# Wider values' projection, an unrolled convolution stage, and h's two parts taken straight from PSUM

## The reference

```python
D_MODEL, SEQ, W_A, W_B, H_A, D_K, CONV_WIDTH = 2048, 512, 1024, 1024, 8, 128, 31
h = rmsnorm(x, pre_norm_g)                      # x: (1, 512, 2048) float32
proj = einsum('btd,dn->btn', h, w_in)           # w_in: (2048, 7168)
q, fz, iv, gate_a, u, ug, gate_b = split(proj)  # each 1024 wide; iv holds the values
o_a = hgrn2_mixer(q, fz, iv, lower_bounds, hg_norm_g) * silu(gate_a)
o_b = conformer_conv(u, ug, dw_kernel, dw_bias, conv_ln_g, conv_ln_b) * silu(gate_b)
y = einsum('btm,md->btd', concatenate([o_a, o_b]), w_out)
out = x + rmsnorm(y, post_norm_g)
```

## Time and profile before

| | us |
|---|---|
| three runs | 893.11, 890.41, 892.97 |
| median | 892.97 |
| the profiled execution, its whole time | 890.29 |
| its span in the profile | 888.3 |
| PE busy in it | 872.4 |
| mean granted clock of PE | 0.992 |

### The profile page before, as it was taken

One profiled execution on the slowest core, in us unless ns is written; L12 is line 12 of the kernel. 1 busy time (PEld: TensorE's weight loads), 2 busy tenths in 40 slices (PEclk: granted clock), 3 DMA queues, 4 the chain that ended last, 5 costly groups with the idle time before them and its releaser, 6 DMA issues.

```text
span 888.3 us, 13244 instructions
## 1 busy us (share of the span) xinstructions
PE 872.4 (98%) x4616; PEld 747.8 (84%) x4616; DVE 567.7 (64%) x911; ACT 386.7 (44%) x585; POOL 363.5 (41%) x165
## 2 busy tenths in 40 slices
PE   6999999999999999999999999999999999999996
PEld 5998898898898888888888888888888888888885
DVE  6877786786786894775849486684948892010105
ACT  6433312312312455654746565573756743222221
POOL 3374444444444444352442435244242534444440
PEclk8999999999999999999999999999999999999999
DMA  9243233233233233132232314233132345433304
GB/s 317 69 128 102 80 104 103 78 104 102 77 105 101 78 95 96 48 116 74 72 94 70 96 47 121 68 88 91 57 94 63 101 140 209 153 100 101 101 5 190
DMA packets 119703, 89.70 MB, mean 101 GB/s; under 512 B 2640, under 2 KB 109433, under 8 KB 118137
## 3 DMA queue, kind: packets, MB, share of 16 engines
q1 hardware_dynamic: 118921, 84.04, 31.1%
q10 hardware_dynamic: 752, 5.25, 1.6%
HBM read 85.09 MB, written 4.19 MB: 101 GB/s over the span
## 4 chain that ended last, share of the span: by engine, by line
PE 96%; DVE 3%; DMA 1%; ACT 0%; DVEq 0%; issue 0%; ACTq 0%
PE banks L1128 19%; PE banks L1126 19%; PE banks L1127 19%; PE banks L1268 7%; PE banks L1267 7%; PE banks L1266 7%; PE banks L1143 3%; PE banks L1142 3%; PE banks L1141 3%; DVE mix L666 1%; PE banks L1187 1%; PE banks L1177 1%; PE banks L1193 1%; PE banks L1221 1%; DVE mix L671 1%; PE banks L1196 1%
## 5 line engine op out<-in xcount | busy, mean ns | idle before, releaser
L324 POOL TENSOR_TENSOR w_lo<-w_raw,w_hi 128x1024 fp32r<-128x1024 f32 x144 | 357.4, 2485 | 497.9 <-ACT w_hi L374 497.8
L1126 PE MATMUL banks<-h_hi,w_hi 128*128 128x512 f32 x736 | 291.2, 396 | 0.0
L1128 PE MATMUL banks<-h_hi,w_lo 128*128 128x512 f32 x736 | 286.7, 390 | 0.0
L1127 PE MATMUL banks<-h_lo,w_hi 128*128 128x512 f32 x736 | 286.6, 389 | 0.0
L374 ACT ACTIVATE w_hi<-w_raw 128x1024 fp32r<-128x1024 f32 x144 | 151.6, 1053 | 260.6 <-PE banks L1268 100.0
L734 DVE SCALAR_TENSOR_TENSOR banks<-work,tap,banks 128x512 f32<-128x512 f32 x232 | 175.3, 756 | 8.0
L1128 PEld LDWEIGHTS banks<-h_hi,w_lo 128*128 128x128 f32 x736 | 138.2, 188 | 29.1
L1127 PEld LDWEIGHTS banks<-h_lo,w_hi 128*128 128x128 f32 x736 | 138.3, 188 | 27.9 <-issue 0.5
L1126 PEld LDWEIGHTS banks<-h_hi,w_hi 128*128 128x128 f32 x736 | 138.3, 188 | 27.8 <-issue 0.5
L1266 PE MATMUL banks<-w_hi,h_hi 128*128 128x512 f32 x256 | 100.6, 393 | 0.0
L1268 PE MATMUL banks<-w_hi,h_lo 128*128 128x512 f32 x256 | 99.7, 389 | 0.0
(11 more groups left out here) (176 smaller groups left out, 927.8 us busy)
## 6 DMA issues: line engine op xcount, KB each, us to landing
w_raw<-in_w_in SPq DMA_DIRECT2D x112, 512.0 KB, 3.7
w_raw<-in_w_out SPq DMA_DIRECT2D x32, 512.0 KB, 3.8
mix<-in_x SPq DMA_DIRECT2D x4, 1024.0 KB, 7.8
work<-in_x ACTq DMA_DIRECT2D x4, 1024.0 KB, 9.8
out_y<-mix SPq DMA_DIRECT2D x3, 1024.0 KB, 3.9
gates<-in_post_norm_g ACTq DMA_DIRECT2D x1, 1024.0 KB, 5.4
out_y<-mix SPq DMA_DIRECT2D x4, 256.0 KB, 2.7
work<-in_dw_kernel SPq DMA_DIRECT2D x1, 64.0 KB
```

What stands on the lines that cost most here:

```text
L324: g.tensor_tensor(w_lo[:, a], w_raw[:, a], w_hi[:, a].bitcast(fp32), ALU.subtract).then_inc(lo_done, 1)
L1126: mm(bank(b), wh, hh, start=kt == 0, stop=False)
L1127: mm(bank(b), wh, hl, start=False, stop=False)
L1128: ins = mm(bank(b), wl, hh, start=False, stop=kt == KT - 1)
```

## The change

Values: `VW` goes from 256 to 512 columns. A unit of values is then 2 channel tiles of the model by 512 columns, 24 products instead of 48; four channels instead of two make one group, and `take_v` copies it out in four pieces, after channel 3 and channel 7. The convolution stage is written out for all 8 channels on SP, ACT and PE (DVE's loop stays).

Head: x's first two tiles are loaded in two pieces each, with two Squares and an Identity that adds the sums. The gain isn't applied by a pass of its own: PE transposes both token tiles of a half into pairs (`x_pair`, 256 columns of one channel tile), ACT writes `h_hi` straight from PSUM with the gain as its scale, DVE writes `h_lo` = PSUM * gain - `h_hi`, both by channel tile (16 pieces per half). DVE takes the squares of tile 2. The warm-up is 20 matmuls of the identity instead of 24 transposes, and 5 more stand between the transposes of tiles 0 and 1. `project_half` runs part by part (hi*hi, then `h_lo`, then `w_lo`), units 0 to 3 of the first token half stand together, and the transposes of tiles 2 and 3 come after them.

```diff
-    WARM = 24
+    WARM = 20
-    VW = 2 * P
+    VH = 4
+    VW = VH * P
     VK = UW // VW
+        def x_pair(th, k):
+            n = k // 2 if th == 0 else 2 + (k // 2) % 6
+            return bank(n)[:, (k % 2) * 2 * P:(k % 2 + 1) * 2 * P]
@@ SP
             def x_load(tt):
+                if tt < 2:
+                    for half in range(2):
+                        a, b = half * UW, (half + 1) * UW
+                        sp.dma_start(mix[:, tt * D + a:tt * D + b], x[0, tt * P:(tt + 1) * P, a:b]).then_inc(x_in[2 * tt + half], 16)
...
-            conv_loads(0, first=True)
-            with sp.Fori(1, J // 2) as i:
-                conv_loads(i)
+            for j in range(J):
+                conv_loads(j)
@@ ACT
+            def x_stats_halves(tt):
+                for half in range(2):
+                    act.wait_ge(x_in[2 * tt + half], 16)
+                    A(gates[:, half * UW:(half + 1) * UW], mix[:, tt * D + half * UW:tt * D + (half + 1) * UW], ACT.Square,
+                      accum_out=ssq[:, 4 + 2 * tt + half:5 + 2 * tt + half]).then_inc(x_sq, 1)
+                act.wait_ge(x_sq, 2 * tt + 2)
+                A(ssq[:, tt:tt + 1], ssq[:, 4 + 2 * tt:5 + 2 * tt], ACT.Identity,
+                  bias=ssq[:, 5 + 2 * tt:6 + 2 * tt]).then_inc(x_ss, 1)
+                x_root(tt)
+            def x_hi_part(th, k):
+                act.wait_ge(x_tr, x_tr_count(th, k))
+                A(h_pair(h_hi, th, k), x_pair(th, k), ACT.Copy, scale=gcol[:, k:k + 1]).then_inc(x_hi, 1)
...
+                for a in range(VH):
+                    A(mix[:, (VH * i + a) * T:(VH * i + a + 1) * T].rearrange("p (c k) -> p c k", k=P),
+                      bank(4, TT).rearrange("p (c n) -> p c n", n=512)[:, :, a * P:(a + 1) * P], ACT.Copy).then_inc(v_taken, 1)
@@ DVE
+            def x_lo_part(th, k):
+                dve.wait_ge(x_hi, KT * th + 2 * (k // 2) + 2)
+                V.scalar_tensor_tensor(h_pair(h_lo, th, k), x_pair(th, k), gcol[:, k:k + 1], h_pair(h_hi, th, k).bitcast(fp32),
+                                       ALU.mult, ALU.subtract).then_inc(x_lo, 1)
             x_scale(0)
-            x_gain(0, 0)
             x_scale(1)
...
+            for k in range(KT):
+                x_lo_part(0, k)
+            dve.wait_ge(x_in[4], 16)
+            V.tensor_tensor_reduce(gates[:, 0:D], mix[:, 2 * D:3 * D], mix[:, 2 * D:3 * D], scale=1.0, scalar=0.0,
+                                   op0=ALU.mult, op1=ALU.add, accum_out=ssq[:, 2:3]).then_inc(x_ss, 1)
             x_scale(2)
             x_scale(3)
+            for k in range(KT):
+                x_lo_part(1, k)
@@ PE
+            def keep_warm(n):
+                for _ in range(n):
+                    mm(OB[:, 3 * P:], ident[:, :], ident[:, :], start=True, stop=True)
...
+            x_transposes(0, 0, 0, KT, False)
+            keep_warm(WARM // 4)
+            x_transposes(0, 1, 0, KT, True)
+            for n in range(RING):
+                project_half(n, 0)
+            pe.wait_ge(x_lo, KT)
+            for k0 in range(0, 12, 4):
+                x_transposes(1, 2, k0, k0 + 4, False)
+                x_transposes(1, 3, k0, k0 + 4, True)
+            pe.wait_ge(x_lo, KT + 4)
+            x_transposes(1, 2, 12, KT, False)
+            x_transposes(1, 3, 12, KT, True)
+            project_half(0, 1)
             pe.wait_ge(par_in, 16 * 7)
+            pe.wait_ge(x_lo, 2 * KT)
```

More of the change, by code:

```diff
@@ L239, in in_unit @@
                 load_unit(n, slot, w_in[0, half * UW:(half + 1) * UW, ds(col, P)], P)
[L241 to L259, removed]
@@ L396, in x_hi_part, with x_root @@
-            def x_hi_part(tt, half):
-                act.wait_ge(x_norm, 2 * tt + half + 1)
-                A(h_half(h_hi, tt, half), x_half(tt, half), ACT.Copy).then_inc(x_hi, 1)
+            def x_root(tt):
+                act.wait_ge(x_ss, tt + 1)
+                A(rst[:, tt:tt + 1], ssq[:, tt:tt + 1], ACT.Ln, scale=1.0 / D, bias=EPSB).then_inc(x_ln, 1)
+                act.wait_ge(x_ln, tt + 1)
+                A(rst[:, tt:tt + 1], rst[:, tt:tt + 1], ACT.Exp, scale=-0.5).then_inc(x_rst, 1)
@@ L406, in _ @@
             hi_unit(1, 1, 0, first=True)
[L407 to L410, removed]
+            for k in range(HK, KT):
+                x_hi_part(0, k)
             hi_unit(2, 2, 0, first=True)
-            x_stats(3)
+            x_root(2)
+            act.wait_ge(x_in[5], 16)
+            A(gates[:, D:2 * D], mix[:, 3 * D:4 * D], ACT.Square, accum_out=ssq[:, 3:4]).then_inc(x_ss, 1)
+            x_root(3)
             hi_unit(3, 3, 0, first=True)
-            for tt in (2, 3):
-                x_hi_part(tt, 0)
-                x_hi_part(tt, 1)
+            for k in range(KT):
+                x_hi_part(1, k)
@@ L446, in conv_channel @@
                         A(glu, glu, ACT.Exp).then_inc(glu_ready, 1)
-            conv_channel(0, 0, True)
-            conv_channel(0, 1, False)
-            with act.Fori(1, J // 2) as i:
-                conv_channel(i, 0, False)
-                conv_channel(i, 1, False)
+            for j in range(J):
+                conv_channel(j)
             def ln_square(j):
@@ L573, in _ @@
                 if u == 0:
[L574 removed]
+                    take_v(GROUPS_V - 1)
                 own(0, u, True)
@@ L1079, in project_half @@
                 v = slice(th * T // 2, (th + 1) * T // 2)
-                pe.wait_ge(x_hi, 4 * th + half + 3)
-                pe.wait_ge(lo_done, n + 1)
-                for lo in range(2):
-                    if lo:
-                        pe.wait_ge(x_lo, 2 * half + 2 if th == 0 else 2 * TT)
+                pe.wait_ge(hi_done, n + 1)
+                for part in range(3):
+                    if part == 2:
+                        pe.wait_ge(lo_done, n + 1)
                     for k in range(HK):
@@ L1113, in _ @@
             nc.tensor.transpose(bank(2)[:, 2 * P:2 * P + last], stage[0:last, 2 * P:3 * P], ident[0:last, 0:last]).then_inc(par_t, 1)
-            project_half(3, 0)
-            for n in range(RING):
+            for n in range(1, RING):
                 project_half(n, 1)
@@ L1156, in conv_channel @@
                     if s >= 4:
-                        if s == 4 and r == 0 and not first:
-                            pe.wait_ge(v_taken, i)
-                        project_values(n, (CONV_U * r + s) % RING, 2 * r + s - 4)
-                    else:
-                        project(n, (CONV_U * r + s) % RING, s % 2, s // 2)
-            conv_channel(0, 0, True)
-            conv_channel(0, 1, False)
-            with pe.Fori(1, J // 2) as i:
-                conv_channel(i, 0, False)
-                conv_channel(i, 1, False)
+                        vu = 2 * (j % VH) + s - 4
+                        if vu == 0 and j:
+                            pe.wait_ge(v_taken, j)
+                        project_values(n, n % RING, vu)
+                    else:
+                        project(n, n % RING, s % 2, s // 2)
+            for j in range(J):
+                conv_channel(j)
             def slot(g, u, first, last=False):
```

148 lines of the change are left out of this document (64 added, 84 removed).

## The result

| | us |
|---|---|
| before, four runs | 893.11, 890.41, 892.97, 892.95; median 892.96 |
| after, four runs | 885.55, 885.01, 885.32, 885.95; median **885.43** |
| ratio | 0.9923 (0.9904 to 0.9941) |
| the profiled execution of after, its time and its span | 885.55, 883.6 |
| values' first product, before and after | 49.07, 49.60 |

The medians differ by 7.5 us where 5.0 was predicted, but the profiled executions by 890.29 - 885.55 = 4.74. The 2.7 us that I had put on the forecast, since before's median stands so much above its profiled execution, aren't there in the changed kernel: its profiled execution lies in the middle of its runs. The median, 885.43, is 2.6 us under the forecast of 888.0.

A forecast was written before the change was run, and what follows sets the result against it. PE bounds the kernel, without a hole from 34.57 us, behind a head waiting on DVE. Profiled 890.29 - 5.0 (values' width) + 0.0 (head even) = 885.3; median 893.0 - 5.0 = 888.0 us, range 884.5 to 891.2.

The forecast's parts named there:

- The 2.7 us that I had put on the forecast: Last step of the sum: the median of the runs stands 2.7 us above the profiled execution, also after the change.
- rival 1: Head: ACT's scale operand is free, 0.28 us per copy; DVE first gives 886.3, POOL first 888.6; chance 0.17.
- rival 3: Head, PE idle between 24.9 and 28.3 us: clock falls, unit 3 and first transposes slow, +2 us, 890.0; chance 0.08.
- Values: Convolution stage: 768 products at 0.120 us go, 384 at 0.227 come, 5.0 us less, all on the path.
- Rival 5: Values: a product of 512 columns costs 0.24 us, so the width gives nothing, 893.0; chance 0.04.
- Convolution stage: Values' copies on ACT stay hidden and the written-out loops cost nothing in sight; bounds 0 to 1 us.
- Start: Head: clock rises at 7.7 us, warm-up lasts until 9.0, scaling starts at 9.6, first four pairs are there at 14.0.
- ACT's pace: Head, pieces of 256 columns with the gain as scale: 0.38 us each, bounds 0.28 and 0.38; eight copies 3.0 us.
- DVE's pace: Head, `h_lo` pieces of 256 columns: 0.34 us each, so DVE follows ACT and ends at 21.9 us.
- DVE first, stall of PE: Head: DVE's squares at 21.8 precede POOL's unit 2 at 22.15; PE stalls 1.5 us, then waits 0.9 for unit 3.
- Rival 2: Head: POOL ahead of DVE's squares at ACT's slow pace, everything behind 2.75 us later, 890.7, no change; chance 0.09.
- rival 4: Head, second half: the low clock stays at 0.50 from 28 us until the values, +12.3 us, 900.3; chance 0.02.

The follow-up runs named there:

- e9b: The changed kernel with unit 3's weights ahead of the two roots and without the five products between the transposes: 882.96 us, ratio 0.9894.
- e10b: e9b with the parameters' three transposes behind unit 1 of the second half instead of ahead of it: 882.08 us, ratio 0.9883.

## Why before has two groups of runs

**Before once more,** the same kernel, to have a profile of the upper group:

> The kernel before once more, unchanged, for the spread of its runs. If its runs lie in two groups (890.4 and 893), the profile shows either: the first values' product at 49.05 us (group of 890.4) or at about 51.7 (group of 893), with the clock's low stretch longer or later than from 14.5 to 24.8 us. If the head has one length only, the 2.7 us are elsewhere and the first values' product starts at 49.05 in both.

Measured: six runs from 890.31 to 890.61 and six from 892.85 to 893.19, and the profiled one, 893.19, is of the upper group. Its values start at 51.99, 2.9 us behind the 49.07 of the execution in the earlier trace rows, and its span is 2.9 us longer (891.2 against 888.3), so these two executions differ in the head alone. In windows of this execution the low clock lies elsewhere:

```profile
9.50:12.90 3.40, 3.39 (x16) 3.27 (x16) 2.00 (x3) 2.67 (x6) 0.64 (x1) 0.50 1.13 359
16.35:26.60 10.25, 7.22 (x33) 6.79 (x33) 10.25 (x10) 7.29 (x9) 1.74 (x2) 0.50 0.77 214
```

The timeline of this execution (893.19):

```profile
9.51 3.62 PE L1071 MATMUL banks<-ident,mix 128*128 128x128 f32 x16 [2.68 <-DVE mix L666]
11.52 1.23 DVE L671 TENSOR_TENSOR mix<-banks,work 128x1024 f32<-128x1024 f32 x1 [1.40 <-PE banks L1071]
12.26 2.36 POOL L324 TENSOR_TENSOR w_lo<-w_raw,w_hi 128x1024 fp32r<-128x1024 f32 x1 [10.20 <-ACT w_hi L374]
12.66 5.27 DVE L666 TENSOR_SCALAR mix<-mix,rst 128x1024 f32<-128x1024 f32 x2
14.86 2.52 POOL L324 TENSOR_TENSOR w_lo<-w_raw,w_hi 128x1024 fp32r<-128x1024 f32 x1 [0.24 <-ACT w_hi L374]
```

and the same rows of the execution that the prediction read (890.29):

```profile
9.34 1.97 PE L1071 MATMUL banks<-ident,mix 128*128 128x128 f32 x16 [2.05 <-DVE mix L666]
10.48 1.22 DVE L671 TENSOR_TENSOR mix<-banks,work 128x1024 f32<-128x1024 f32 x1 [0.53 <-PE banks L1071]
11.62 3.51 DVE L666 TENSOR_SCALAR mix<-mix,rst 128x1024 f32<-128x1024 f32 x2
12.00 5.36 POOL L324 TENSOR_TENSOR w_lo<-w_raw,w_hi 128x1024 fp32r<-128x1024 f32 x2 [9.94 <-ACT w_hi L374]
```

With the granted clock at 0.50, the level of 1.2 GHz, the 16 transposes take 3.62 instead of 1.97 us. They also start 0.17 us later, so the gain pass comes 1.04 us later and ends behind POOL's request. In the good case DVE's first scaling has the access, POOL's first unit waits for it, and DVE's second half waits for one unit (3.51 us for both). In the bad case DVE asks while POOL's first unit runs (12.66 against 12.26), waits for it, and then its second half waits for POOL's second unit: 5.27 us. The scaling is then 5.27 - 3.51 = 1.76 us longer. Together 1.04 + 1.76 = 2.8 us, and 2.9 are seen at the values. So the slower transposes account for about 1 us, and the turned order of two engines for the larger part.

The kernel with the new values and the old head has a profile of its lower group (885.07), and there the clock was low soon after these transposes began:

```profile
10.28:13.70 3.42, 3.06 (x16) 2.69 (x15) 3.21 (x3) 3.35 (x6) 1.70 (x1) 0.50 1.10 392
```

```profile
11.63 3.51 DVE L661 TENSOR_SCALAR mix<-mix,rst 128x1024 f32<-128x1024 f32 x2
12.00 5.36 POOL L322 TENSOR_TENSOR w_lo<-w_raw,w_hi 128x1024 fp32r<-128x1024 f32 x2 [9.94 <-ACT w_hi L372]
```

The first eight transposes, for which the gain pass waits, were done by then; DVE asked first, and the scaling took its 3.51 us. The straight stage's profile (890.37, lower group) is the same: low from 10.32 us, DVE at 11.66, POOL at 12.23. So a stretch of low clock in the head doesn't by itself make the upper group. Of the upper group there is one profile, and in it the stretch lay over the first transposes.

**POOL's first unit behind the scaling.** If that order is the whole cause, forcing it should leave the lower group alone:

```diff
+            pool.wait_ge(x_scaled, 4)
             for n in range(PEEL * RING):
                 lo_unit(n, n % RING)
```

> The kernel before; POOL's first unit also waits until tile 1 is scaled (x_scaled 4). A: the two groups of the kernel before (890.4 and 893.0) come from DVE's scaling of tile 1 having to wait for one unit of POOL or for two, which a clock low during the first transposes decides. With POOL behind the scaling, the wait is gone: no run near 893, all runs at or below 890.4, down to about 888.5, and what spread is left is the 1 us of the slower transposes. B: the groups come from the low clock itself (half-speed products of units 0 to 2): then they stay 2.6 us apart.

Measured: 12 runs from 889.67 to 893.34, in no groups, median 891.14; ratio 0.9995 (0.9984 to 1.0006). The kernel didn't settle at the lower group, so the theory "no run near 893, all at or below 890.4" fell, and so did the other, that the groups stay 2.6 us apart. In the profiled run, the longest (893.34), the timeline says:

```profile
12.13 1.41 DVE L667 TENSOR_SCALAR mix<-mix,rst 128x1024 f32<-128x1024 f32 x2
13.68 4.71 POOL L324 TENSOR_TENSOR w_lo<-w_raw,w_hi 128x1024 fp32r<-128x1024 f32 x2 [11.62 <-DVE mix L667]
16.85 8.24 DVE L678 TENSOR_TENSOR h_lo<-mix,h_hi 128x1024 fp32r<-128x1024 f32 x4
```

The scaling is free of POOL (1.41), but POOL's two units are later and meet DVE's next operations with two SBUF inputs: the subtractions take 8.24 us and not the 4.54 of the earlier trace rows. The wait was moved, not taken away. In this run the clock was also at 0.50 from 27.0 to 33.9 us, and 16 transposes at 28.02 took 3.65 us, which is a part of its 893.34. So the order of DVE and POOL is shown in the profiles as what sets the two groups apart, and the groups are gone where the order is forced; but this run is no clean proof, since it made new meetings. What spreads its runs over 3.7 us isn't shown, nor a cheap cure in the old head.

## What bounds the new head

These edits are to the changed kernel. Between batches its median moved by 0.6 us (885.43 and, below, 884.79), so steps smaller than that are read within a batch. The warm-up's 20 products took 7.04 us in the profile above and between 6.08 and 7.63 in those of its variants, as the clock rose earlier or later, which also moves the start of the head; where it matters, it is said.

**ACT without the memory operand.** The gain is left out of `h_hi`:

```diff
-                A(h_pair(h_hi, th, k), x_pair(th, k), ACT.Copy, scale=gcol[:, k:k + 1]).then_inc(x_hi, 1)
+                A(h_pair(h_hi, th, k), x_pair(th, k), ACT.Copy).then_inc(x_hi, 1)
```

> The changed kernel with ACT's copies to h_hi without the gain as scale (h_hi is then the normed x without its gain; h_lo is still PSUM times gain minus h_hi). A: the operand from memory costs ACT 0.09 to 0.1 us a piece: pieces 0.27 to 0.28 us apart instead of 0.356. DVE's pace of 0.39 then is the longer one, and POOL's third unit is asked for before DVE's squares: POOL first, the squares wait some 2.3 us, the head ends up to 1 us later than in the changed kernel, 885.5 to 886.5. B: the operand is free: 0.356 stays, nothing moves.

Measured: 887.48 (886.41 to 888.23); ratio 0.9951 (0.9931 to 0.9971). Two microseconds **slower** than 885.43, with less work. Timeline:

```profile
17.25 2.40 ACT L413 ACTIVATE h_hi<-banks 128x256 fp32r<-128x256 f32 x8
20.66 2.40 POOL L328 TENSOR_TENSOR w_lo<-w_raw,w_hi 128x1024 fp32r<-128x1024 f32 x1 [0.75 <-ACT w_hi L378]
21.17 4.04 DVE L696 CUSTOM_DVE_ANT_0 gates<-mix 128x2048 f32<-128x2048 f32 x1
...
29.24 2.07 PE L1099 MATMUL banks<-h_hi,w_hi 128*128 128x256 f32 x8 [3.72 <-ACT w_hi L378]
```

and the window behind the hole:

```profile
28.20:35.00 6.80, 5.76 (x27) 5.77 (x28) 1.42 (x2) 0.98 (x2) 2.66 (x1) 0.50 0.25 74
```

Eight copies take 2.40 us and not the 3.07 of the changed kernel: the scale operand costs 0.08 us per copy of 256, so my choice of 0.38 over 0.28 held: they start 0.37 us apart with it and 0.29 without. But DVE, at 0.39 us a piece, couldn't follow: its last piece ended at 21.24 us, ACT's at 19.65. POOL, which hangs on ACT's weight copy, was first, and now the squares waited (4.04 us). Tile 3's chain and unit 3 came later, PE stood idle for 3.72 us, and the granted clock fell to 0.50 from 28.2 us: unit 3's three parts then took 5.49 us. That is the second case of rival 1 (ACT fast, POOL first) and rival 3 of the prediction, both seen in a neighbour of the kernel. The profiled run, 888.23, is the longest of the four, and 0.55 us of it lie at the start, where the clock rose later (first copy at 14.18 against 13.63). The Trainium skill (SBUF — State Buffer, "Who interferes with whom") has the engine that issues first keep the shared ports for its whole instruction. By that rule 20.66 before 21.17 makes the squares wait until 23.06 and end 2.2 us later, at 25.2, and the trace agrees: 21.17 + 4.04 = 25.21.

**Unit 3's weights ahead of tile 2's and 3's roots.** The chain says that unit 3 waits for two roots which it doesn't need:

```diff
             hi_unit(2, 2, 0, first=True)
+            hi_unit(3, 3, 0, first=True)
             x_root(2)
...
             x_root(3)
-            hi_unit(3, 3, 0, first=True)
```

> The changed kernel, ACT's copy of unit 3's weights moved ahead of the root of tile 2 and the squares of tile 3. ACT is idle there for 2.4 us. A: PE's wait of 0.7 us for w_hi of unit 3 and of 1.0 us for its w_lo go, the second half's transposes start about 1.5 us earlier, and the runs lie near 884.0. B: POOL's unit 3, asked for at once behind unit 2, holds the shared ports when DVE wants to scale tiles 2 and 3, and the scaling becomes what the transposes wait for: 0 to 0.5 us gained, or up to 1 us lost.

Measured: 883.62 (883.05 to 884.26); ratio 0.9911 (0.9894 to 0.9927), 1.8 us less than 885.43. The timeline, and under it the chain, of this kernel:

```profile
21.99 7.30 POOL L328 TENSOR_TENSOR w_lo<-w_raw,w_hi 128x1024 fp32r<-128x1024 f32 x2 [1.47 <-ACT w_hi L378]
```

```profile
21.99 4.50 POOL w_lo L328
26.53 4.09 PE banks L1099 x32
```

Unit 3 doesn't wait any more, and PE streams from 26.53 to 30.63. From the start of the squares to the values it is 26.21 us (21.95 to 48.16), against 28.09 in the changed kernel (21.51 to 49.60): 1.9 us less, free of what the start does. The hole ahead of it, POOL behind DVE's squares, stays.

**Without the five products between the transposes:**

```diff
             x_transposes(0, 0, 0, KT, False)
-            keep_warm(WARM // 4)
             x_transposes(0, 1, 0, KT, True)
```

> The changed kernel without the five fp32 products between the transposes of tiles 0 and 1 (20 at the start stay). A: they are on the chain from 11.98 to 13.10 us and only keep the clock: without them all of the head's chain is 1.1 us earlier, near 884.4, since PE has other work beside them. B: the clock's grant falls in some runs, which then are 1 to 3 us slower, in two groups.

Measured: 884.90 (884.25 to 885.14); ratio 0.9924 (0.991 to 0.9939). That is 0.5 us under 885.43, less than the two medians of the changed kernel differ, so it isn't settled by this run alone. In its profile the warm-up took 7.62 us and not 7.04, since the clock rose later, and still the first copy starts at 13.17 and not 13.63: 0.58 + 0.46 = 1.04 us, close to the 1.1 of theory A. Behind the squares nothing changes (21.06 to 49.17, 28.11 us). The clock didn't fall for want of the five.

## Towards a better version

One batch, with the changed kernel in it again. **The changed kernel:**

> The changed kernel once more, for the spread of its runs: one group between 885.0 and 886.0, no run 2 us or more above the others. If DVE's squares and POOL's third unit, asked for 0.03 us apart in the profile, came in either order from run to run, a second group 2 to 3 us higher would stand beside it.

Measured: 884.79 (884.71 to 885.59); ratio 0.9917 (0.9902 to 0.9931). No run stands 2 us above the others, as expected; three lie 0.2 to 0.3 us under the lower bound. Squares at 21.48, POOL at 21.52.

**Both edits from above together:**

> The changed kernel with the edits of e6 (unit 3's weights ahead of the two roots) and e7 (no five products between the transposes). A: the five products are on the chain in both, so their 1.1 us, less what the warm-up's own end moves, add to e6's: near 883.0. B: POOL's third unit behind DVE's squares is what bounds now, and it moves with the chain as well, so the same; if the clock falls in some runs, those are 2 us slower.

Measured: 882.96 (882.80 to 883.12), 1.8 us less; ratio 0.9894 (0.9877 to 0.9911); values start at 47.18. How the 1.8 us divide between the two edits, no run of this batch shows; from the squares on it is 26.20 us, as with unit 3's edit alone.

**And the parameters' transposes later,** so that a unit with all its inputs fills the time in which PE waits for `h_lo`'s last piece:

```diff
             project_half(0, 1)
+            project_half(1, 1)
...
-            for n in range(1, RING):
+            for n in range(2, RING):
```

> e9b with the parameters' three transposes (which wait for all of h_lo) behind unit 1 of the second half instead of ahead of it. A: PE's wait of 1.0 us for DVE's last pieces is filled with unit 1's first products, which need only its own pieces: 0.9 to 1.0 us less than e9b, near 882.1. B: the parameters come 2.9 us later to DVE and ACT, and the weight copy of unit 4 behind them (ACT waits for the lower bounds' chain first) makes PE wait at the first values' product, near 48 us: nothing gained or up to 2 us lost, with a hole in PE there.

Measured: 882.08 (881.75 to 882.10), 0.9 us less again; ratio 0.9883 (0.9866 to 0.9901); values start at 46.09.

**And tile 2's squares on ACT,** so that DVE doesn't stand in POOL's way:

```diff
             hi_unit(2, 2, 0, first=True)
+            act.wait_ge(x_in[4], 16)
+            A(gates[:, 0:D], mix[:, 2 * D:3 * D], ACT.Square, accum_out=ssq[:, 2:3]).then_inc(x_ss, 1)
             x_root(2)
+            hi_unit(3, 3, 0, first=True)
...
-            dve.wait_ge(x_in[4], 16)
-            V.tensor_tensor_reduce(gates[:, 0:D], mix[:, 2 * D:3 * D], mix[:, 2 * D:3 * D], scale=1.0, scalar=0.0,
-                                   op0=ALU.mult, op1=ALU.add, accum_out=ssq[:, 2:3]).then_inc(x_ss, 1)
```

> e10b with the squares of tile 2 on ACT (where it was idle) instead of DVE, ahead of unit 3's weights. A: DVE's squares and POOL's unit 2 no longer exclude each other: POOL's unit 2 takes 2.4 us instead of 4.5, PE doesn't wait for it, and the second half's transposes start 1.0 to 1.4 us earlier: near 881. B: the root of tile 3 comes later (about 27.8 us) and its scaling waits for POOL's unit 3 until 28.2: gain under 0.5 us.

Measured: **880.61** (880.42 to 880.80); ratio 0.9869 (0.9852 to 0.9886); values start at 44.55. It is 1.5 us less again, 4.2 less than the changed kernel of its batch, and 12.3 less than before's median, 892.93 (9.9 less than the lower group's 890.5). The edit does two things, since unit 3's weights now stand behind tile 2's root. Timeline and chain:

```profile
20.63 2.41 POOL L328 TENSOR_TENSOR w_lo<-w_raw,w_hi 128x1024 fp32r<-128x1024 f32 x1 [1.46 <-ACT w_hi L378]
24.34 2.41 POOL L328 TENSOR_TENSOR w_lo<-w_raw,w_hi 128x1024 fp32r<-128x1024 f32 x1 [1.31 <-ACT w_hi L378]
```

```profile
14.60 13.44 PE banks L1098 x96
...
29.82 1.67 DVE h_lo L685 x4
```

Both of POOL's units take 2.41 us, and the whole first half, 96 products in the chain, is PE's from 14.60 to 28.04. What is left is the step from the first to the second token half.

## Why the prediction was right, and where it wasn't

The time lies in the range, 884.5 to 891.2, and the two halves of the mechanism, 5 us from the width and a head that is even with the good course of the old one, are what the runs show. But 885.43 is just under the range of the forecast itself, 885.5 to 890. The whole range reached so low only for rival 1 with an early clock, and rival 1 didn't happen, so it is in part luck that the median fell inside. The sum for the profiled execution held; the step from it to the median didn't.

**The term that failed is the last one of the sum:** "The median of the runs stands 2.7 us above that execution, so the median after is 893.0 - 5.0 = 888.0 us." The sum for the profiled execution was 885.3, and 885.55 was measured. The 2.7 us were read as something that lies on any kernel. The runs show that they are a second course of the old head, 2.6 us longer, into which 21 of 29 runs fell, and in which the profiled execution wasn't. Here the new head's 9 runs (884.71 to 885.95), and the 12 with 256 columns, lie within 1 us each. In its profile DVE asked for the scaling of tile 1 at 11.13 us, 1.13 ahead of POOL's first unit (12.26), and it took its 1.42 us without a wait. I had three runs, 893.11, 890.41 and 892.97, two close together and one 2.6 us away, and the profiled execution beside the one: they showed it, and I took a median.

Point by point, for the profiled execution:

- *Values.* Predicted 5.0, measured 5.2 to 5.3. 384 products at 0.227 us stand in place of 768 at 0.120. From the first values' product to the end of the last it is 244.62 us before (49.07 to 293.69) and 239.39 after (49.60 to 288.99), 5.23 less. Summed over the trace, the distances between starts give 92.11 and 87.07 us for the values, 5.04 less; the other 0.19 lie in the 672 products of 512 columns between them (152.51 and 152.32). Why, isn't shown. An estimate from the figures of the Trainium skill (TensorE: Matmul & The Clock Gate, "Wait — 56ns, not 53.3ns?") gave 1.0; the runs decide against it. Rival 5 fell.
- *Convolution stage.* Nothing, as predicted: the straight stage alone shows it, and PE has no hole from 49.60 us to its last product at 875.60.
- *Start.* The warm-up's records start 0.213 us apart up to 6.6 us and 0.112 behind that, so the clock was up at 6.6 instead of 7.7, within the bound given (two such records are one plain fp32 product of 128 columns, 0.22 us; an fp32r product of 256 columns takes 0.120); scaling from 9.14 instead of 9.6, first copy at 13.63 instead of 14.0.
- *ACT's pace.* 3.07 us for eight where 3.0 was said. Right, and the run without the operand shows why.
- *DVE's pace.* Wrong: 0.39 us a piece and not 0.34. With PSUM, a gain from memory and `h_hi` as inputs, 16 pieces take 6.36 us. In the first half DVE ends 1.08 us behind ACT (21.60 and 20.52) where 0.8 was said, and of DVE's lead over POOL, 0.35 us in the prediction, 0.03 were left. In the second half it is DVE and not ACT that binds (6.37 us in the chain), and PE waits 0.83 us for its last piece at 40.37.
- *DVE first, stall of PE.* Right in order: 1.19 us where 1.5 was said, and 0.52 + 0.87 = 1.39 for unit 3 where 0.9 was. (The DVE operation of the earlier trace rows didn't end with POOL but 0.55 us behind it, at 429.66 against 429.11: it waited, and then ran.) The end of the first half is 32.08 against 31.85, the values 49.60 against 49.1. The head "is even" to 0.5 us in this profile, and 0.3 by the runs with 256 columns.
- *Rival 1* (free operand) fell. *Rival 2* (POOL first at ACT's slow pace) didn't happen in either profile of this kernel, but by 0.03 us. *Rivals 3 and 4* (clock): none in this kernel; 1.7 us idle between 24.8 and 27.8 didn't bring the clock down, 3.7 us of it in one piece in the run without the operand did, and it was back at 35 us, so of rival 4 nothing was seen.

## What to carry to other kernels

Before a median is taken as the base of a sum, look at the runs: two values with nothing between are two courses of the kernel, and a change must be costed against each of them, with the profile placed in its group. Where two engines exclude each other, write down for each meeting who asks first and by how much: a small margin is a term of some microseconds, and a faster producer can turn it to the loss. Work that PE needs goes ahead of work that only a later stage needs, on every engine in between.

## What was unexpected in the hardware

- The clock can cost more through order than through speed: with eight transposes at the low level ahead of it the gain pass came 1.04 us later, and with the order that this turned the end came 2.6 to 2.9 us later.
- The margin between DVE and POOL was 0.03 or 0.04 us in all seven profiles in which DVE takes the squares and ACT keeps its scale, though the meeting as a whole lay anywhere from 20.90 to 21.95 us. Both requests hang on ACT, so they move together.
- A DVE operation with a square, a sum and one SBUF tile read twice (2048 columns, 2.28 us) excludes POOL like the plain two-input ones: it took 4.04 us behind POOL, and POOL's unit, 2.4 us alone, took 4.48 behind it.
